# A four-layer decoder in split fp32: buffers at 64-byte multiples, MLP up products in runs, and another order at the mixer ends and MLP entries

## The reference

```
for i in range(4):
    h = rmsnorm(x, norm_mix[i])
    y = hgrn2_mixer(h, ...) if i % 3 == 0 else moba_mixer(h, ...) if i % 3 == 1 else pool_mixer(h, ...)
    x = x + y
    a = relu(rmsnorm(x, norm_mlp[i]) @ w1[i])        # 1024 x 4096
    x = x + (a * a) @ w2[i]                          # 4096 x 1024
return rmsnorm(x, norm_final)
```

## Time and profile before

| | us |
|---|---|
| median of 3 runs | 1243.08 (1243.03 to 1243.19) |
| profiled execution: its own time | 1242.63 |
| its span in the trace | 1240.5 |
| PE busy | 1191.4 (96%) |
| DVE busy | 792.3 (64%) |
| ACT busy | 672.6 (54%) |

### The profile page before, as it was taken

One profiled execution on the slowest core, in us unless ns is written; L12 is line 12 of the kernel. 1 busy time (PEld: TensorE's weight loads), 2 busy tenths in 40 slices (PEclk: granted clock), 3 DMA queues, 4 the chain that ended last, 5 costly groups with the idle time before them and its releaser, 6 DMA issues.

```text
span 1240.5 us, 17170 instructions
## 1 busy us (share of the span) xinstructions
PE 1191.4 (96%) x6851; PEld 1037.3 (84%) x6851; DVE 792.3 (64%) x798; ACT 672.6 (54%) x793; POOL 47.7 (4%) x40
## 2 busy tenths in 40 slices
PE   6999899999999999999998899999988989999998
PEld 5999897888889989888886788888887988888886
DVE  6787756655656656755655875566778775655563
ACT  5955556444544444544455554455786555644543
POOL 4000000000001001000001100000100000000000
PEclk9999999999999999999999999999999999999999
DMA  9443234654455435555626455546434223555450
GB/s 346 151 136 102 97 108 170 207 200 167 171 206 185 144 114 166 178 200 180 217 96 222 149 204 200 207 139 208 142 122 136 103 93 113 170 203 204 148 207 34
DMA packets 85000, 202.90 MB, mean 164 GB/s; under 512 B 3293, under 2 KB 5415, under 8 KB 84688
## 3 DMA queue, kind: packets, MB, share of 16 engines
q1 hardware_dynamic: 84912, 202.10, 47.1%
q0 software_dynamic: 32, 0.02, 0.0%
HBM read 201.04 MB, written 1.06 MB: 163 GB/s over the span
## 4 chain that ended last, share of the span: by engine, by line
PE 80%; DVE 8%; ACT 6%; issue 3%; DMA 2%; POOL 0%; SPq 0%; ACTq 0%; DVEq 0%; POOLq 0%
PE acc L621 9%; PE acc L620 9%; PE acc L622 9%; PE misc L588 9%; PE hb L588 9%; PE misc L589 4%; PE hb L589 4%; PE hb L529 3%; PE hb L531 3%; PE hb L532 3%; DVE wlo L1349 3%; PE acc L724 2%; ACT whi L979 2%; PE hb L544 2%; PE hb L546 2%
## 5 line engine op out<-in xcount | busy, mean ns | idle before, releaser
L1349 DVE TENSOR_TENSOR wlo<-raw,whi 128x2048 fp32r<-128x2048 f32 x186 | 427.0, 2325 | 184.8 <-ACT whi L979 184.7
L979 ACT ACTIVATE whi<-raw 128x2048 fp32r<-128x2048 f32 x186 | 347.7, 1905 | 117.9 <-PE acc L622 101.5
L620 PE MATMUL acc<-whi,arena_r 128*128 128x512 f32 x512 | 202.6, 396 | 0.0
L621 PE MATMUL acc<-wlo,arena_r 128*128 128x512 f32 x512 | 202.3, 395 | 0.0
L622 PE MATMUL acc<-whi,arena_r 128*128 128x512 f32 x512 | 202.1, 395 | 0.0
L588 PE MATMUL hb<-xhl,whi 128*128 128x512 f32 x512 | 183.2, 400 | 5.3 <-DVE arena L1768 3.0
L588 PE MATMUL misc<-xhl,whi 128*128 128x512 f32 x512 | 182.9, 399 | 4.0 <-DVE arena L1750 2.0
L589 PE MATMUL misc<-xhl,wlo 128*128 128x256 f32 x512 | 143.7, 281 | 0.0
L589 PE MATMUL hb<-xhl,wlo 128*128 128x256 f32 x512 | 143.7, 281 | 0.0
L588 PEld LDWEIGHTS hb<-xhl,whi 128*128 128x128 f32 x512 | 96.2, 188 | 30.6 <-DVE arena L1768 3.8
L588 PEld LDWEIGHTS misc<-xhl,whi 128*128 128x128 f32 x512 | 96.2, 188 | 29.0 <-DVE arena L1750 2.3
(11 more groups left out here) (251 smaller groups left out, 1833.2 us busy)
## 6 DMA issues: line engine op xcount, KB each, us to landing
raw<-in_mlp_w_dram SPq DMA_DIRECT2D x128, 1024.0 KB, 5.4
raw<-in_a_w_in_dram SPq DMA_DIRECT2D x32, 1024.0 KB, 5.5
raw<-in_b_w_qkv_dram SPq DMA_DIRECT2D x12, 1024.0 KB, 7.5
raw<-in_a_w_out_dram SPq DMA_DIRECT2D x8, 1024.0 KB, 5.1
raw<-in_b_w_out_dram SPq DMA_DIRECT2D x4, 1024.0 KB, 5.1
arena<-in_x_dram SPq DMA_DIRECT2D x1, 1024.0 KB, 5.2
arena<-in_decay_dram SPq DMA_DIRECT2D x1, 1024.0 KB, 11.8
arena<-bias_rows SPq DMA_DIRECT2D x1, 1024.0 KB, 6.0
```

Of the source, the lines that this page charges most:

```text
L620: pe.matmul(o, ys, h, start=first and kt == 0, stop=False, skip_group_check=True)
L621: pe.matmul(o, ys, l, start=False, stop=False, skip_group_check=True)
L979: act.activation(whi[:, g % 2, u, 0:n], raw[:, g % 2, u, 0:n], ACT.Copy).then_inc(hi_done, 1)
L1349: dve.tensor_tensor(wlo[:, g % 2, u, 0:n], raw[:, g % 2, u, 0:n], whi[:, g % 2, u, 0:n].bitcast(F32), ALU.subtract).then_inc(lo_done, 1)
```

## The change

1. **Layout.** `arena` and `arena_r` are allocated right after `xhl`, and now start at 147584 and 198784, both multiples of 64 bytes. The small tensors come after them; `rstd`, `ident`, `ones` and `decay` stay at multiples of 64.
2. **Up products.** For a tile, all wide matmuls come first and then all narrow ones. In the first up group of a layer, the four tiles' wide matmuls of a half come first and wait only for `hi_done`, then the narrow ones, after a wait for `lo_done`.
3. **Banks.** `out_banks` and `up_pairs` begin with the `misc` banks instead of `hb`, so `out_half(0, 0)` and `out_half(1, 0)` write banks that the norm of `o` has read, and the wait for `bank_free` stands behind them.
4. **HGRN2's end.** `quad_outputs(1)` comes one quarter earlier, and `oms_step(2)` and `(3)` come after quarter 14 instead of inside the output projection. The split of the output projection's first group ends in quarter 12, and that of its second group lies around the last gate and norm steps in another order.
5. **MLP entry.** In layers 0, 1 and 3 the second unit of the first up group is split earlier on ACT, and on DVE after all of `take_x`. In all layers the first unit of `g + 2` is split inside the first `hidden`.

```diff
+        arena = sb("arena", [P, 12800])
+        arena_r = sb("arena_r", [P, 4096], F32R)
         rstd = sb("rstd", [P, SEQ])
...
-        out_banks = [hb[0], hb[1], misc[0], misc[1]]
+        out_banks = [misc[0], misc[1], hb[0], hb[1]]
...
-        up_pairs = [hb_pair, misc_pair]
+        up_pairs = [misc_pair, hb_pair]
...
                 if r_at is None:
                     for half in range(2):
+                        kts = range(4 * half, 4 * half + 4)
+                        pe.wait_ge(hi_done, lo_at + half + 1)
                         for f in range(4):
                             if half == 0:
                                 pe.wait_ge(x_ready, 4 * (2 * layer + 1) + 1 + f)
-                            mm = tile(f, 4 * half, 4 * half + 4)
+                            for kt in kts:
+                                wide(f, kt)
+                        pe.wait_ge(lo_done, lo_at + half + 1)
+                        for f in range(4):
+                            for kt in kts:
+                                mm = narrow(f, kt)
                             if half and f % 2:
                                 mm.then_inc(bank_ready, 1)
                     return
                 for i in range(2):
                     pe.wait_ge(summed, r_at + (i - 1))
                     for q in range(2):
-                        mm = tile(2 * i + q, 0, KT)
+                        for kt in range(KT):
+                            if i == 0 and q == 0 and kt % 4 == 0:
+                                pe.wait_ge(lo_done, lo_at + (kt // 4 + 1))
+                            wide(2 * i + q, kt)
+                        for kt in range(KT):
+                            mm = narrow(2 * i + q, kt)
                     mm.then_inc(bank_ready, 1)
...
-                            12: lambda: (oms_step(0), oms_step(1)), 13: lambda: quad_outputs(1)}
+                            12: lambda: (quad_outputs(1), oms_step(0), oms_step(1)),
+                            14: lambda: (oms_step(2), oms_step(3))}
...
+                    out_half(0, 0)
+                    out_half(1, 0)
                     pe.wait_ge(bank_free, free_count(layer) + 12)
-                    out_half(0, 0)
-                    oms_step(2)
-                    oms_step(3)
-                    out_half(1, 0)
                     out_half(2, 0)
                     out_half(3, 0)
...
-                take_x(n + 1, {} if layer % 3 == 2 else {1: lambda: split_unit(g, 0), 5: lambda: split_unit(g, 1)})
+                take_x(n + 1, {} if layer % 3 == 2 else {1: lambda: split_unit(g, 0), 3: lambda: split_unit(g, 1)})
...
                         if first and i == 0:
                             rms(n + 1)
+                            split_unit(g + 2, 0)
...
-                take_x(n + 1, mixed, {} if layer % 3 == 2 else {1: lambda: split_unit(g, 0), 2: lambda: split_unit(g, 1)})
+                if layer % 3 == 2:
+                    take_x(n + 1, mixed)
+                else:
+                    take_x(n + 1, mixed, {1: lambda: split_unit(g, 0)}, (0, 1))
+                    split_unit(g, 1)
```

More of the change, by code:

```diff
@@ L188, in build_decoder @@
         ident_r = sb("ident_r", [P, P], F32R)
-        arena = sb("arena", [P, 12800])
-        arena_r = sb("arena_r", [P, 4096], F32R)
         def carve(at, *dims):
@@ L578, in mlp_up, with wide, narrow @@
             def mlp_up(layer, g, lo_at, r_at=None):
-                def tile(f, k0, k1):
-                    o = out_banks[f]
-                    for kt in range(k0, k1):
-                        need_x(2 * layer + 1, kt)
-                        if f == 0 and kt % 4 == 0:
-                            pe.wait_ge(lo_done, lo_at + (kt // 4 + 1))
-                        h, l = (w_k(t, g, kt, f * P, (f + 1) * P) for t in (whi, wlo))
-                        pe.matmul(o[:, :], h, xhl[:, kt, :, :], start=kt == 0, stop=False, skip_group_check=True)
-                        mm = pe.matmul(o[:, 0:SEQ], l, xh[:, kt, :], start=False, stop=kt == KT - 1,
-                                       skip_group_check=True)
-                    return mm
+                def wide(f, kt):
+                    need_x(2 * layer + 1, kt)
+                    return pe.matmul(out_banks[f][:, :], w_k(whi, g, kt, f * P, (f + 1) * P), xhl[:, kt, :, :],
+                                     start=kt == 0, stop=False, skip_group_check=True)
+                def narrow(f, kt):
+                    return pe.matmul(out_banks[f][:, 0:SEQ], w_k(wlo, g, kt, f * P, (f + 1) * P), xh[:, kt, :],
+                                     start=False, stop=kt == KT - 1, skip_group_check=True)
                 if r_at is None:
                     for half in range(2):
+                        kts = range(4 * half, 4 * half + 4)
+                        pe.wait_ge(hi_done, lo_at + half + 1)
                         for f in range(4):
@@ L1176, in _ @@
                     for quarter in range(16):
-                        if quarter % 2 == 0:
+                        if quarter % 2 == 0 and quarter < 14:
                             split_unit(g0 + 5 + quarter // 4, quarter // 2 % 2)
@@ L1192, in _ @@
                             gate_silu_a(quarter // 2 - 5)
-                        if quarter in (11, 13, 15):
+                        if quarter == 12:
+                            split_unit(out0, 1)
+                        if quarter in (11, 13):
                             gate_silu_b()
@@ L1198, in _ @@
                             cross_copy(1)
-                        if quarter == 12:
+                        if quarter == 13:
                             o_rstd(0)
                             o_rstd(1)
-                        if quarter == 13:
+                            o_squares(2)
+                            o_squares(3)
                             o_hi(0)
                             o_hi(1)
+                        if quarter == 14:
+                            o_rstd(2)
+                            gate_silu_b()
+                    split_unit(out0 + 1, 0)
                     gate_silu_a(3)
-                    o_squares(2)
-                    o_squares(3)
+                    o_rstd(3)
                     gate_silu_b()
-                    split_unit(out0 + 1, 0)
-                    o_rstd(2)
-                    o_rstd(3)
-                    split_unit(out0 + 1, 1)
                     o_hi(2)
                     o_hi(3)
+                    split_unit(out0 + 1, 1)
                 elif layer % 3 == 1:
@@ L1282, in _ @@
                 hidden(0, b, r0, first=True)
-                split(g + 2)
+                split_unit(g + 2, 1)
                 hidden(1, b + 2, r0 + 2)
@@ L1354, in split, with take_x @@
                     split_unit(g, u, it, n)
-            def take_x(n, update, between={}):
+            def take_x(n, update, between={}, early=()):
                 def lo(f):
@@ L1366, in take_x @@
                     update(k)
-                    if k % 2:
-                        for f in range(2 * k - 2, 2 * k + 2):
+                    if k == 0:
+                        for f in early:
                             lo(f)
@@ L1371, in take_x @@
                         between[k]()
+                    if k % 2:
+                        for f in range(2 * k - 2, 2 * k + 2):
+                            if f not in early:
+                                lo(f)
             def column(n):
@@ L1776, in hidden @@
                                                  op0=ALU.max, op1=ALU.mult).then_inc(scaled_done, 1)
+                        if first and i == 0:
+                            split_unit(g + 2, 0)
                         dve.wait_ge(hh_done, r_at + (i + 1))
```

7 lines of the change are left out of this document (4 added, 3 removed).

## The result

| | before | changed |
|---|---|---|
| time, median (lowest to highest) of 4 runs | 1243.05 us (1240.97 to 1243.19) | 1220.54 us (1219.86 to 1221.41) |
| span of the profiled execution | 1240.5 us | 1217.7 us |
| its own time | 1242.6 us | 1219.86 us |

The ratio is 0.9821, with a 95% interval from 0.9805 to 0.9836: 22.5 us faster, where 28 were forecast. The forecast was 1215.0, its range 1210 to 1223.

A forecast was written before the change was run, and what follows sets the result against it. PE's own pace was taken to bound the loop, with few waits elsewhere. Terms of -8.6, +1.4, -4.5, -11.9 and -4.0 summed to -27.6 us from 1242.6, giving 1215; range 1210 to 1223.

The forecast's parts named there:

- runs bring nothing: Up products: a pair of wide and narrow matmuls stays at 352.8 ns, total 1220 us; chance 14%.
- Part 1, layout: Aligned buffers: 512-column down slots 6.4 ns quicker, -8.6 us; 256-column output and decay products slower, +1.4 us.
- Its main term: MLP down groups: 1344 slots that PE alone bounds, each 6.4 ns quicker, -8.6 us.
- neither: Neither buffer starts nor reordered up products shorten a matmul slot; gain only from waits and clock, 1227 us; chance 6%.
- Parts 3 and 4, HGRN2's end: Layers 0 and 3: the wait before the output projection and the clock's fall go, 6.8 and 5.1 us, together -11.9.
- layer 0's 3.4 us for the fall: Layer 0's output projection: half of at least 6.70 us at the 1.2 GHz clock is saved.
- The steps laid out by hand: HGRN2's end: split and norm steps ready at 155.7, 161.3 and 164.8 us, before PE wants them; smallest margin 1.5 us.
- Part 2, runs: Up groups: wide matmuls in a row, then narrow ones, save 6.1 ns on each of 736 pairs, -4.5 us.
- part 5, entries: MLP entries of layers 0 to 3 change by -2.5, +0.5, +1.0 and -3.0 us, together -4.0.
- I take 6.1: Up products: a wide and narrow pair falls from 352.8 to 346.7 ns, a gain of 6.1; other bound 0.
- Both halves of the first up group run through, and `ones_mm` 0.9: Layer 0's MLP entry: first up group 11.1 us without a wait, plus 0.9 for the ones product, 12.0.
- The new waits: MLP entry, layer 0: PE waits 1.1 us inside the second up group and 1.0 for `wlo` in the third.

The follow-up runs named there:

- sum first: Changed kernel plus one DVE wait for POOL's sum of squares ahead of the split of the MLP's second group; 1218.69 us, ratio 0.9799 to the kernel before.

## Why the prediction was right, and where its terms were off

**Direction and mechanisms** held part by part. It came out 5.5 us long of the forecast, and inside the range. The time alone would also fit the first rival, *runs bring nothing* (1220); the up group of 11.15 us rules that out, though the runs' net gain of 1.6 us comes near it.

**Part 1, layout** (-7.2): 7.1 in the run that has it alone, and right in its reason: down slots at 227 ns, output products at 120.0. Its main term was somewhat large, 0.31 us for a down group where the loop gave 0.25 alone and 0.29 in the changed kernel. The rival *neither* falls. The Trainium skill, "TensorE: Matmul & The Clock Gate", Step-by-step, says that loading the next tile's weights takes no read bandwidth from the running matmul. The time of 1227 that the prediction drew from it does not come out: a slot does depend on where the tile starts whose weights are loaded, 233.1 against 227.1 ns. By which path it does, no run shows.

**Parts 3 and 4, HGRN2's end** (-11.9): 10.6. Both waits and both falls of the clock went. The term was 0.6 too large by its own rows: layer 0's 3.4 us for the fall is half of a stretch of 6.7 us, but PE was busy for only 5.58 of it and stood in the wait for the rest, which was counted already; half of 5.58 is 2.8. The steps laid out by hand ended about 1 us late (156.6, 162.6 and 166.0 instead of 155.7, 161.3 and 164.8), and PE still waited for none.

**Part 2, runs, and part 5, entries** (-4.5 and -4.0): here the sum failed, 4.0 together instead of 8.5. Two steps were at fault.
- "I take 6.1" a pair. The loop gave (11.29 - 11.15) / 32 = 4.4, because a wide run behind a narrow one costs 230 ns a slot and not 226.7. That the runs cost something at the entries was charged, 0.5 and 1.0 us in layers 1 and 2, and is about right: at this count the runs cost 0.5 and 1.2 there.
- "Both halves of the first up group run through, and `ones_mm` 0.9": this step left POOL out. The entry puts three splits in a row on DVE, they stop POOL's sum, and the first up group with its wait takes 11.98 us where it takes 11.13 without, in three layers, with `rstd`, `hl` and the splits behind it. The two runs that take this away gain 2.7 and 2.9 us.

The entries, from the first up product to the end of the first tile of the third up group as in the prediction, in us:

| layer | before | forecast | changed | sum first |
|---|---|---|---|---|
| 0 | 41.3 | 38.8 | 39.6 | 38.6 |
| 1 | 38.4 | 38.9 | 39.4 | 38.6 |
| 2 | 40.1 | 41.1 | 41.0 | 41.0 |
| 3 | 43.3 | 40.3 | 41.4 | 40.5 |
| sum | 163.1 | 159.1 | 161.4 | 158.6 |

The entries gained 1.7 us where 4.0 were forecast. The difference stands in layers 0, 1 and 3, where POOL's sum is long, and with the sum ahead of the splits every layer comes within 0.3 us of the forecast. The sign was in the trace before, in rows that I did not read. Timelines of POOL and DVE, kernel before, layer 0:

```profile
179.02 2.83 POOL L1860 TENSOR_TENSOR hn<-hn 128x512 f32<-128x512 f32 x1 [123.32 <-ACT hn L998]
189.03 1.30 POOL L1863 TENSOR_TENSOR hn<-hn 128x512 f32<-128x512 f32 x1 [7.18 <-ACT hn L998]
```

```profile
178.42 2.28 DVE L1349 TENSOR_TENSOR wlo<-raw,whi 128x2048 fp32r<-128x2048 f32 x1
```

The first of two equal sums took 1.5 us longer. It began inside this split and ended 1.15 us behind it (181.85 and 180.70), as the others do.

**The new waits** that I named came at their places. In layer 0 PE stood still for 194.60 - (192.72 + 0.96) = 0.92 us where 1.1 was forecast, and for 212.73 - (211.21 + 4 x 0.227) = 0.61 where 1.0 was.

**What the difference is made of.** The profiled executions differ by 22.8 us, 4.8 less than the 27.6 of the sum. The entries make 2.3 of them. The slots make 2.2: 0.06 us for each of 23 steady up groups and 0.03 for each of 28 down groups. The clock in layer 2 makes none. Its stretch at 1.2 GHz at 668.6 us is 6.8 us long and the one before, at 681.5, is 3.4, but both lie inside the mixer, and from layer 1's last down group to layer 2's first up product PE takes 45.4 us now and 45.7 before. Over thirteen profiles this time is 45.3 to 46.0 us, in no order by the length of the fall.

## What to carry to other kernels

Look at the start address of the tile that a matmul takes as its stationary operand: two `sb` lines in another order were worth a third of this change. Reordering matmuls changes when each operand is first asked for, so a better pace in the loop has to be paid where operands arrive late, and its waits should be set anew for each kind of matmul. When splits or other two-input work are packed together on DVE, check what POOL has to read in that stretch. An account by stage, between the same matmuls of both traces, tells where a forecast was missed, and whether a fall of the clock cost anything.

## What the runs showed that was not expected

- A start 32 bytes off a multiple of 64 costs a 512-column fp32r matmul 6 ns in its stationary operand (233.1 against 227.1 ns), while as moving operand it made a 256-column one 1.7 ns quicker (118.3 against 120.0).
- DVE's `tensor_tensor` of two SBUF tiles stops POOL's across several instructions: POOL got no turn between three splits in a row.
- Taking work off no engine, one added wait on DVE made the kernel 2.7 us faster by the ratios.
- The reordering that gains 0.11 us on each steady up group (11.29 to 11.18) made the whole kernel 4.7 us slower by itself, and 1.6 us faster together with the other parts.
